# Falls of the eight levels of a gated linear recurrence, from one running sum on POOL in place of a matrix product per level

## The reference, cut to what matters

```python
f = lb + (1.0 - lb) * jax.nn.sigmoid(z)
log_f = jnp.log(jnp.maximum(f, F_FLOOR))
k = (1.0 - lb) * jax.nn.sigmoid(-z)
...
b = jnp.cumsum(lfb, axis=2)
diff = b[:, :, :, None, :] - b[:, :, None, :, :]
decay = jnp.where(tri, jnp.exp(jnp.where(tri, diff, 0.0)), 0.0)
attn = jnp.einsum('bhtd,bhsd,bhtsd->bhts', qb, kb, decay)
o = jnp.einsum('bhts,bhsv->bhtv', attn, vb) + jnp.einsum('bhtd,bhdv->bhtv', qb * jnp.exp(b), state)
```

## Time and profile before

| | us |
|---|---|
| median of 3 runs | 1976.78 |
| lowest, highest | 1975.28, 1978.91 |
| the profiled execution | 1978.37 |
| its span, first to last instruction | 1976.5 |
| granted clock of PE, mean over the span | 0.987 of full |

### The profile page before, as it was taken

How to read it: one execution, slowest core, us unless ns; L and a number is a source line. 1 busy time by engine, 2 the same in 40 slices (tenths; PEclk the granted TensorE clock), 3 DMA queues, 4 the chain that set the end, 5 groups by cost and what they waited for, 6 DMA issues and landing times. The chain is left out here.

```text
span 1976.5 us, 29280 instructions
## 1 busy us (share of the span) xinstructions
PE 1908.6 (97%) x13178; PEld 958.2 (48%) x13178; DVE 410.7 (21%) x837; ACT 287.7 (15%) x566; POOL 41.1 (2%) x57
## 2 busy tenths in 40 slices
PE   7999999999999999999799999999999999999996
PEld 4476654457744454577444344443444434344342
DVE  3633323213410000235311010110101111010121
ACT  1210220223310000332211010110101001010110
POOL 0100000001000000010000000000000000000000
PEclk9999999999999999999899999999999999999998
DMA  9732227334124353441559999999999999999990
GB/s 279 255 122 87 86 77 249 112 131 170 43 99 174 110 182 111 142 152 68 205 200 385 353 389 380 355 384 355 387 380 360 382 356 383 364 378 381 367 402 35
DMA packets 221663, 485.83 MB, mean 246 GB/s; under 512 B 14492, under 2 KB 27420, under 8 KB 221405
## 3 DMA queue, kind: packets, MB, share of 16 engines
q1 hardware_dynamic: 213472, 472.02, 65.3%
q10 hardware_dynamic: 6702, 7.03, 1.2%
q0 software_dynamic: 1360, 4.85, 0.6%
HBM read 475.74 MB, written 8.14 MB: 245 GB/s over the span
## 5 line engine op out<-in xcount | busy, mean ns | idle before, releaser
L1288 PE MATMUL bank<-ring,work 128*128 128x512 f32 (+4 forms) x1632 | 675.1, 573 | 18.5 <-ACT work L1502 3.6
L1288 PEld LDWEIGHTS bank<-ring,work 128*128 128x128 f32 x1632 | 307.1, 193 | 357.9 <-issue 324.6
L2758 PE MATMUL bank<-ring,work 128*64 128x512 f32 x1792 | 396.9, 595 | 0.6 <-DVE work L2900 0.6
L2758 PEld LDWEIGHTS bank<-ring,work 128*64 128x64 f32 x1792 | 123.6, 137 | 239.6 <-issue 238.7
L2766 PE MATMUL bank<-ring,work 128*32 128x256 f32 x3584 | 205.0, 381 | 0.0
L2804 PE MATMUL bank<-ring,work 128*64 128x512 f32 x896 | 204.6, 599 | 0.0
L2766 PEld LDWEIGHTS bank<-ring,work 128*32 128x32 f32 x3584 | 110.8, 110 | 112.6 <-issue 45.4
L2929 DVE TENSOR_TENSOR work<-work,bank 64x512 f32<-64x512 f32 x56 | 38.7, 691 | 374.8 <-ACT work L2848 374.8
L2804 PEld LDWEIGHTS bank<-ring,work 128*64 128x64 f32 x896 | 59.3, 136 | 117.0 <-issue 117.0
L2813 PE MATMUL bank<-ring,work 128*32 128x256 f32 x1792 | 108.3, 382 | 0.0
L2813 PEld LDWEIGHTS bank<-ring,work 128*32 128x32 f32 x1792 | 52.6, 110 | 74.2 <-issue 45.4
(11 more groups left out here) (355 smaller groups left out, 1151.9 us busy)
## 6 DMA issues: line engine op xcount, KB each, us to landing
ring<-in_moe_w_gate SPq DMA_DIRECT2D x56, 2048.0 KB, 10.4
ring<-in_moe_w_up SPq DMA_DIRECT2D x56, 2048.0 KB, 9.4
ring<-in_moe_w_down SPq DMA_DIRECT2D x56, 2048.0 KB, 13.0
ring<-in_w_in SPq DMA_DIRECT2D x20, 2048.0 KB, 8.1
ring<-in_w_out SPq DMA_DIRECT2D x6, 2048.0 KB, 8.9
ring<-in_dense_w_gate SPq DMA_DIRECT2D x5, 2048.0 KB, 8.5
ring<-in_dense_w_up SPq DMA_DIRECT2D x5, 2048.0 KB, 7.8
ring<-in_dense_w_down SPq DMA_DIRECT2D x5, 2048.0 KB, 7.9
```

The lines of the kernel that those rows point to most:

```text
L1288: mm = pe.matmul(banks(j)[:, 0:width], x[:, k0 + kt, tt * P:(tt + 1) * P], w[:, kt, c0:c0 + width], start=first and n == 0, stop=last and ...
L2758: mm = pe.matmul(out[half, :], xgT[:, k, 0:64], w[n][:, k, :], start=(k == 0), stop=(k == KD - 1))
```

## The change: what it does

PE multiplies only once per layer: `m.lf` by `incl`, the running sum within each 64 tokens. ACT copies the two banks back over `m.lf`, now turned and summed. POOL, in a new `falls(n)`, forms the falls of each level from it: differences with the value at the middle token (levels 0 to 5 two subtractions a tile; level 6, whose halves are the 64 tokens themselves, a subtraction and a copy; level 7 adds the chunks' ends). They go to `m.e[n % 2]`, and ACT's exp runs in place there. New semaphores: `falls_ready` (POOL to ACT) and `falls_raised` (ACT to DVE, in place of "bank left"). POOL does falls 0 to 3, then the rope, then falls 4 to 7; falls(n) for n of 2 and more waits for `sides(n - 2)`, whose input it overwrites. The seven squares `decay{n}`, `after` and `upto` go; `incl` comes: 8 DMAs in place of 16.

```diff
-    def use_sums(n):
-        for tt in range(NT):
-            J["sums", n, tt] = banks.new("scalar")
-
-    use_sums(0)
+    for tt in range(NT):
+        J["sums", tt] = banks.new("scalar")
...
-        def sums(n):
+        def sums():
             for tt in range(NT):
-                j = J["sums", n, tt]
+                j, mask = J["sums", tt], sq["incl"]
                 banks.enter(pe, j)
-                mask = sq[f"decay{n}"] if n < LEVELS else sq["after" if tt == 0 else "upto"]
...
-            if n + 1 < n_levels:
-                sums(n + 1)
...
         def fall(n):
             for tt in range(NT):
-                j = J["sums", n, tt]
-                act.wait_ge(*banks.ready(j))
-                if n >= 2:
-                    act.wait_ge(*m.sides_ready.at(2 * (n - 2) + tt + 1))
-                banks.leave(nc.scalar.activation(m.e[n % 2][:, tt, :], banks(j)[:, :], ACT.Exp), j)
+                e = m.e[n % 2][:, tt, :]
+                act.wait_ge(*m.falls_ready.at(2 * n + tt + 1))
+                m.falls_raised.give(nc.scalar.activation(e, e, ACT.Exp))
...
-        act.wait_ge(*m.decays_ready.at(2))
+        for tt in range(NT):
+            copy(J["sums", tt], m.lf[:, tt, :], banks(J["sums", tt])[:, :])
         fall(0)
...
+        def falls(n):
+            half = 1 << n if n < LEVELS else CH
+            for tt in range(NT):
+                out, b = (x[:, tt, :].rearrange("p (h two s) -> p h two s", two=2, s=half) for x in (m.e[n % 2], m.lf))
+                if n >= 2:
+                    pool.wait_ge(*m.sides_ready.at(2 * (n - 2) + tt + 1))
+                pool.wait_ge(*banks.left(J["sums", tt]))
+                pairs = 512 // (2 * half)
+                middle = b[:, :, 0, half - 1].unsqueeze(2).broadcast_to([P, pairs, half])
+                if n < LEVELS:
+                    pool.tensor_tensor(out[:, :, 0, :], middle, b[:, :, 0, :], ALU.subtract)
+                    if n + 1 < LEVELS:
+                        last = pool.tensor_tensor(out[:, :, 1, :], b[:, :, 1, :], middle, ALU.subtract)
+                    else:
+                        last = pool.tensor_copy(out[:, :, 1, :], b[:, :, 1, :])
+                elif tt == 0:
+                    end = b[:, :, 1, half - 1].unsqueeze(2).broadcast_to([P, pairs, half])
+                    step(pool.tensor_tensor(out[:, :, 0, :], middle, b[:, :, 0, :], ALU.subtract))
+                    pool.tensor_tensor(out[:, :, 0, :], out[:, :, 0, :], end, ALU.add)
+                    last = pool.tensor_tensor(out[:, :, 1, :], end, b[:, :, 1, :], ALU.subtract)
+                else:
+                    pool.tensor_copy(out[:, :, 0, :], b[:, :, 0, :])
+                    last = pool.tensor_tensor(out[:, :, 1, :], b[:, :, 1, :], middle, ALU.add)
+                m.falls_ready.give(last)
...
-                dve.wait_ge(*banks.left(J["sums", n, tt]))
+                dve.wait_ge(*m.falls_raised.at(2 * n + tt + 1))
...
-        hgrn_names = [f"decay{n}" for n in range(LEVELS)] + [f"pick{n}" for n in range(LEVELS)] + ["after", "upto"]
+        hgrn_names = ["incl"] + [f"pick{n}" for n in range(LEVELS)]
```

More of the change, by code:

```diff
@@ L87, in constant_squares @@
         pair = (row // (2 * half)) == (col // (2 * half))
-        right = (col // half) % 2 == 1
-        middle = (col // (2 * half)) * 2 * half + half - 1
-        sq[f"decay{n}"] = np.where(right, (row > middle) & (row <= col), (row > col) & (row <= middle))
         sq[f"pick{n}"] = pair & ((row // half) % 2 == 0) & ((col // half) % 2 == 1)
@@ L1697, in __init__ @@
          self.sides_ready, self.rope_turned, self.kpe_ready, self.max_ready, self.probs_ready, self.value_roots,
-         self.values_scaled, self.gate_gained, self.bound_spread, self.bound_ready) = self.signals = [new(n) for n in (
+         self.values_scaled, self.gate_gained, self.bound_spread, self.bound_ready, self.falls_ready,
+         self.falls_raised) = self.signals = [new(n) for n in (
              "latent_roots", "latents_scaled", "clamped", "logs", "decays_ready", "sides_ready",
              "rope_turned", "kpe_ready", "max_ready", "probs_ready", "value_roots", "values_scaled", "gate_gained",
-             "bound_spread", "bound_ready")]
+             "bound_spread", "bound_ready", "falls_ready", "falls_raised")]
     def passed(self):
@@ L1746, in mixer_stage @@
     for n in range(n_levels):
-        if n + 1 < n_levels:
-            use_sums(n + 1)
         if n == 0:
@@ L1896, in _ @@
         pe.wait_ge(*m.decays_ready.at(2))
-        sums(0)
+        sums()
         pe.wait_ge(*banks.left(J["kT", 0]))
@@ L2124, in _ @@
             m.gate_gained.give(pool.tensor_tensor(rows, rows, wide(core.out_norms[:, layer, :], HH), ALU.mult))
+        def falls(n):
[22 more added lines that the diff above has]
+                m.falls_ready.give(last)
+        falls(0)
+        falls(1)
+        falls(2)
+        falls(3)
         pool.wait_ge(*banks.left(J["qr"]))
@@ L2139, in _ @@
         m.rope_turned.give(pool.tensor_copy(out[:, :, 5, :], out[:, :, 4, :]))
+        for n in range(4, n_levels):
+            falls(n)
     @core.block.vector
```

## The result

| | before | changed |
|---|---|---|
| median of the runs, us | 1977.76 (4 runs, 1975.28 to 1978.91) | 1957.18 (4 runs, 1954.39 to 1960.56) |
| ratio | | 0.9898 [0.9877, 0.9920] |
| profiled execution, us | 1978.37, span 1976.5 | 1955.08, span 1953.2 |

The change saves 20.6 us by the medians (16 to 24 us by the interval of the ratio) and 23.3 us between the two profiled executions. The forecast was a gain of 22.7 us, or 1954.0 us.

A forecast was written before the change was run, and what follows sets the result against it. PE's own instruction stream was taken as the bound: 25.1 us of removed products less 2.4 us of waits coming back gives 22.7 us, from the median 1976.78 to 1954.0 us. Forecast case 1951.5 to 1957, full range 1951 to 1962.

The forecast's parts named there:

- What PE gets back: PE's recurrence: 7 groups of 16 `sums` products a layer go at 1.79 us each, 12.5 us a layer, 25.1 for both.
- Logits 0: Level 4: PE waits for DVE's copies of `spun`, idle 2.2 us in place of 1.73, +0.5 us a layer.
- `mixed(0)`: Level 5: PE gets there at 509.66, ahead of ACT's copy of probs 0 at 509.9, +0.3 us a layer.
- `mixed(2)`: Levels 6 and 7: DVE reaches softening 3 some 0.3 to 0.4 us after PE is ready, +0.4 us a layer.
- POOL at nothing: POOL's 33 new operations a layer, 0.63 us each (range 0.52 to 1.27), stay hidden and cost nothing.
- POOL's room: Ahead of logits 0: falls 4 ready at 485.1, allowed until 490.0; 4.9 us of room, used up at 0.88 us an operation.
- the turn-taking: DVE and POOL hinder each other: each `sides` beside POOL delays POOL by 4 x 0.34 = 1.3 us.
- Squares, banks, ACT's copies: Small edits: 3.8 us less issuing on SP gains nothing, banks only loosen waits, ACT's two copies are counted in POOL's chain.
- Does it reach the end: Behind the recurrence: everything shifts whole, since SP's loads for the experts wait for PE; experts start 23 us earlier.
- The rival of the experts' stream: Experts: DMA is the true bound there and layer 1's gain is lost in waits for weights, 1965.4 us; chance 0.03.
- forecast case: Whole run: the gain of 22.7 us holds, 1951.5 (nothing given back on PE) to 1957 us; chance 0.75.
- POOL late by a few us: Falls 4 on POOL: operations of 1.0 to 1.1 us come 2.4 to 4.4 us late, 1959 to 1963 us; chance 0.14.

The follow-up runs named there:

- Experiment 1: Changed kernel with the 8 products of the scores issued twice in levels 0 to 6: 1979.38 us, ratio 1.0007 to the kernel before.
- experiment 6: Changed kernel with the turning of the `spun` rows and their copies moved ahead of `scores(3)` and `pick(3)`, on PE and DVE: 1951.43 us, ratio 0.9868.
- experiment 7: Changed kernel with two swaps on ACT, `probs(0)` ahead of `fall(6)` and `probs(2)` ahead of `soft(3)`: 1957.53 us, ratio 0.9893.
- experiments 2 and 3: Changed kernel with each POOL falls operation but level 7's in-place addition doubled, 1974.93 us; with only the first of each tile's falls doubled, 1958.58 us.
- experiment 4: Changed kernel with the falls formed on DVE instead of POOL, which keeps the rope: 1957.33 us, ratio 0.9909.
- experiment 5: Changed kernel with 8 more, unused squares loaded on SP's queue, 16 in all as before: 1956.43 us, ratio 0.9895.

## Why the prediction was right

- **What PE gets back.** Forecast 12.5 us a layer from PE's pitch. Experiment 1 puts the pitch back and has the old time. The recurrence of layer 0 is 11.23 us shorter, so 12.5 - 11.23 = 1.3 us came back in waits, where 1.2 was forecast.
- **The three waits.** Logits 0: from 1.73 to 2.01, +0.3 (forecast +0.5). The chain was right: the pick ends 0.93 after `scores(3)` and the copies take 1.95. The 0.2 too much come from two measures mixed: the 2.2 of the forecast was counted from start to start, the 1.73 is the idle time that the profile shows behind overlapping records. With 0.65 us for the six turnings (490.46 to 491.11 in experiment 6) the wait is 503.18 - 500.64 - 0.65 = 1.9 before and 491.91 - 489.08 - 0.65 = 2.2 after. `mixed(0)`: 498.56 instead of 498.39, where PE would have been, +0.2 (forecast +0.3). `mixed(2)`: idle for 0.65, and 0.80 by the starts (505.99 - 503.40 less the 1.79 of `scores(6)`; 0.06 before), where +0.4 was forecast, the weakest of the three estimates. The copy of probs 2 stands behind softening 3 on ACT, which idles 2.01 us for DVE's maxima; experiment 7 takes this wait away by putting the copy first.
- **POOL at nothing.** Forecast 0.63 us an operation at every level, taken between 0.52 and 1.27; it is 0.61, and 0.79 beside DVE. From start to start it is 0.57 against DVE's 0.34, 1.7 times. The rule on strided reads in the Trainium skill (GPSIMD Engine Reference, section "Performance pitfalls for Q7 kernels"), which by its letter adds nothing up to 8 bytes, agrees with level 0's 0.61; no run has a step of over 8 bytes.
- **POOL's room.** The limit of 30.5 us came out as 30.0 (experiments 2 and 3); the arrival was forecast 1.8 us too late. Three terms make this up. The 20 operations cost 0.57 each from start to start and not 0.63, 1.2 us less. I had each `sides` beside POOL cost POOL four times 0.34, 4.0 us in all outside the rope; in fact a DVE operation (0.34 a start) and a POOL operation (0.57) together take 0.76, less than the sum of 0.91, so each pair cost POOL 0.19, and the whole was 2.1. Against that, a wait was missing in the sum: POOL stood idle for 1.4 us ahead of the rope, whose input DVE had still to copy from a bank (its start at 470.94).
- **Who loses by the turn-taking.** DVE's 9.3 us more of busy time appear in no wait of PE's: the one wait for DVE in the recurrence is the copies' own 1.95 us behind the pick. In experiment 4, where the falls no longer stretch `sides`, that wait is the same 2.01.
- **Squares, banks, ACT's copies.** Nothing, as forecast; experiment 5 shows it for the squares. Banks and copies had no experiment of their own; no wait of PE in the recurrence names them but the two above.
- **Does it reach the end.** It does: 59.91 and 956.67 us behind the recurrence, against 60.21 and 956.66. The rival of the experts' stream is out.
- **What the sum left out.** The half clock behind the wait in one of two layers, 1.67 us. I read the 2.2 us as idle time only and did not ask what the clock does behind it. With it the forecast would be 22.7 - 1.67 = 21.0, near the medians' 20.6; but their interval, 16 to 24 us, holds both, so only the profiles tell. That the two profiled executions lie 23.3 us apart, close to 22.7, is luck: 2.63 too much from the first 300 us, 1.67 too little by the half clock. The median of 1957.18 lies 0.2 above the forecast case's own range of 1951.5 to 1957, and within the full range.
- **The rivals.** POOL late by a few us, the next likeliest, would have given 1959 to 1963. The median comes near it, but the trace speaks against it: POOL finishes falls 4 6.2 us ahead of its limit. A time alone could not have told these two apart.

Left open: what decides whether PE falls to half clock behind a wait, in the recurrence as in the first 300 us. For the two given kernels the 2.63 us are traced to two such places; for the other profiles it is shown only that their spread, 456.5 to 466.2 us, arises ahead of the last 161.5 us.

## What to carry to other kernels

When one engine's stream is the bound, a product removed is worth its start-to-start pitch, but it was also cover: find for each consumer the copy or exp that it hid, and subtract what now shows. The cheapest gain is often beside the one sought: a wait whose producer and consumer are queued with nothing between them on PE, and with something unrelated between them on DVE, costs its length in every layer, and it went away by moving six instructions on each of the two. Whether an off-path engine bounds anything is told by doubling its work, not by its share of busy time; and a time's agreement with a forecast should be checked in lengths of one stage, since the noise of another stage (here 2.6 us in the first 300 us) is as large as a term.

## What the hardware did that I had not expected

- **Half the clock after 2.0 us.** PE was at 2.4 GHz, stood idle for 2.0 us within a busy stream, and in 7 of 14 cases then ran at 1.2 GHz for between 3 and 4 us (granted clocks of 0.85, 0.50 and 0.79 in the three stretches of 2 us above), at a cost of 1.67 us. So such a wait costs 2.0 or 3.7 us, and which of the two could not be foretold.
- **POOL does not mind short runs.** A subtraction of 128x256 with one operand repeated takes 0.61 us with runs of 1 to 64 elements.
- **DVE and POOL overlap in part.** Two-input operations with all inputs in SBUF cost 0.76 us for a pair, one on each engine, not the sum of 0.57 + 0.34 = 0.91. The Trainium skill (SBUF — State Buffer, section "SBUF: two separate sides") has the later one blocked for the whole of the other's instruction, which by these pitches would be 0.91; the measurement decides, and it shows a part of them overlapped. The section names DVE operations with two inputs in SBUF as the ones that collide, and there the trace agrees: the picks, with one input in a bank, were not slowed.
